# Final-state stores moved to SyncE's queue and sample value products merged by pairs, in a two-layer hybrid decoder step

## The reference, cut to what matters

```python
def block(x, lp, st, ffn_fn, ffn_p):
    mix, new_st = mixer(rmsnorm(x, lp['n1']), lp, st)
    x = x + mix @ lp['w_out']
    x = x + ffn_fn(rmsnorm(x, lp['n2']), *ffn_p)
    return x, new_st
```

```python
    s = jnp.einsum('nthd,ntjhd->nthj', q.astype(F32), kg) * (Dh ** -0.5)
    ...
    o = jnp.einsum('nthj,ntjhd->nthd', p, vg) / den[..., None]
    new_buf = jnp.concatenate([buf, jnp.stack([k, v], axis=2).astype(buf.dtype)], axis=1)[:, T:]
```

## Time and profile before

| what | value |
|---|---|
| median of 3 runs | 1847.91 us |
| the profiled execution | 1849.23 us |
| its span, first to last instruction | 1847.0 us |
| PE busy / DVE / ACT / POOL | 1687.7 / 954.0 / 696.2 / 391.3 us |
| mean granted TensorE clock | 0.936 of full speed |
| mixer's end of layer 0 / layer 1 | about 306 to 352 us / 1088 to 1133 us |

### The profile page before, as it was taken

How to read it: one execution, slowest core, us unless ns; L and a number is a source line. 1 busy time by engine, 2 the same in 40 slices (tenths; PEclk the granted TensorE clock), 3 DMA queues, 4 the chain that set the end, 5 groups by cost and what they waited for, 6 DMA issues and landing times.

```text
span 1847.0 us, 33779 instructions
## 1 busy us (share of the span) xinstructions
PE 1687.7 (91%) x13514; PEld 1625.7 (88%) x13514; DVE 954.0 (52%) x1433; ACT 696.2 (38%) x1050; POOL 391.3 (21%) x236
## 2 busy tenths in 40 slices
PE   6999978799999999998999877859999999999993
PEld 5999857789999999998998567859999999999993
DVE  5577676532210122226776765255746548457474
ACT  4533363342221223235333633443534435335342
POOL 4300250343443344443002503030000000000031
PEclk8999986699999999999999877969999999999997
DMA  4222227422222223222222212368778678677682
GB/s 176 81 70 77 74 72 266 188 80 92 92 87 86 81 92 105 79 81 69 69 77 78 70 50 86 112 211 277 241 246 288 217 255 290 216 266 259 234 313 75
DMA packets 71225, 271.42 MB, mean 147 GB/s; under 512 B 11668, under 2 KB 12404, under 8 KB 70300
## 3 DMA queue, kind: packets, MB, share of 16 engines
q1 hardware_dynamic: 63988, 250.52, 39.7%
q10 hardware_dynamic: 3464, 10.62, 1.8%
q0 software_dynamic: 3648, 8.53, 1.3%
HBM read 253.24 MB, written 36.34 MB: 157 GB/s over the span
## 4 chain that ended last, share of the span: by engine, by line
PE 81%; DVE 7%; POOL 4%; issue 3%; ACT 2%; DMA 1%; ACTq 0%; DVEq 0%; POOLq 0%; SPq 0%
PE psum L1189 39%; PE psum L1709 11%; PE psum L1719 10%; PE psum L1711 9%; PE psum L1236 9%; POOL r_cvt L674 2%; POOL r_w L676 1%; PE psum L1688 1%; PE psum L1241 1%; PE psum L1677 1%; DVE n L1780 1%; POOL r_cvt L675 1%; DVE r_bt L1964 0%; DVE acc L1767 0%; DMA wraw<-in_w_in 0%
## 5 line engine op out<-in xcount | busy, mean ns | idle before, releaser
L1709 PE MATMUL psum<-xg,xhi 128*128 128x320 f32 x1408 | 371.4, 307 | 1.2 <-issue 0.9
L1711 PE MATMUL psum<-xg,xlo 128*128 128x256 f32 x1408 | 369.7, 282 | 0.0
L637 POOL TENSOR_TENSOR wlo<-wraw,whi 128x1024 fp32r<-128x1024 f32 (+1 forms) x90 | 231.3, 2572 | 405.0 <-ACT whi L777 405.0
L1709 PEld LDWEIGHTS psum<-xg,xhi 128*128 128x128 f32 x1408 | 265.2, 188 | 3.5 <-issue 3.1
L1711 PEld LDWEIGHTS psum<-xg,xlo 128*128 128x128 f32 x1408 | 265.3, 188 | 0.0
L1189 PE MATMUL psum<-xnh,whi 128*128 128x260 f32 x1120 | 234.6, 291 | 32.1 <-POOL xnl L694 12.5
L777 ACT CAST whi<-wraw 128x1024 fp32r<-128x1024 f32 (+1 forms) x130 | 140.7, 1085 | 288.4 <-DMA wraw<-in_w_in 161.9
L415 DVE TENSOR_TENSOR xlo<-xraw,xhi 128x1024 fp32r<-128x1024 f32 x176 | 215.2, 1224 | 54.3 <-ACT xhi L1137 54.2
L1137 ACT CAST xhi<-xraw 128x1024 fp32r<-128x1024 f32 x176 | 182.7, 1048 | 142.1 <-PE psum L1711 142.0
L1189 PE MATMUL psum<-xnl,whi 128*128 128x260 f32 x1120 | 228.3, 286 | 0.0
L1189 PE MATMUL psum<-xnh,wlo 128*128 128x260 f32 x1120 | 228.2, 286 | 0.0
(11 more groups left out here) (427 smaller groups left out, 2422.1 us busy)
## 6 DMA issues: line engine op xcount, KB each, us to landing
xraw<-in_moe_gu SPq DMA_DIRECT2D x176, 512.0 KB, 4.2
xraw<-in_moe_dn SPq DMA_DIRECT2D x64, 704.0 KB, 5.8
wraw<-in_w_in SPq DMA_DIRECT2D x54, 512.0 KB, 3.2
wraw<-in_ffn_gu SPq DMA_DIRECT2D x44, 512.0 KB, 3.2
wraw<-in_ffn_dn SPq DMA_DIRECT2D x16, 704.0 KB, 4.1
wraw<-in_w_out SPq DMA_DIRECT2D x16, 512.0 KB, 3.5
out_cache_s<-in_cache SPq DMA_DIRECT2D x4, 2040.0 KB
rows_in<-in_zero SPq DMA_DIRECT2D x8, 640.0 KB, 33.8
```

What stands on the lines that cost most here:

```text
L637: pool.tensor_tensor(wlo[u % RAW][:, 0:cols], wraw[u % RAW][:, 0:cols], whi[u % SPL][:, 0:cols].bitcast(F32), ALU.subtract).then_inc(lo_ma ...
L1709: pe.matmul(epart(n), xhi[n % HIX][:, k * P:(k + 1) * P], xg[:, k, :], start=(k == 0), stop=False, skip_group_check=True)
L1711: ins = pe.matmul(epart(n)[:, 0:256], xlo[n % RWX][:, k * P:(k + 1) * P], xg[:, k, 0:256], start=False, stop=(k == KD - 1), skip_group_che ...
```

## The change

Four edits:

- The six state stores are taken off ACT's list in `sample` and put on SP's, behind a wait for PE's job `mt` 2 and ahead of the cache shifts (layer 0) or the gain tables (layer 1).
- `wv` is moved ahead of the outputs of heads 2 and 3 on PE and in the table of jobs; with that the bank of `wv` and of the next nine jobs changes.
- The 64-row and the 16-row product of each sample become one of 80 rows by 2 x 2 columns: 16 products for 24. For that the probabilities of group 2 go to columns of their own in `spw` (16 columns wider), the rest of these columns is cleared once by POOL, and ACT makes one more small copy per layer.
- DVE adds the result of `wv` (two instructions) before the third `normalise` and not after the last `mean_squares`.

ACT still waits for `state_out` at the end of `sample`, as before.

```diff
@@ mixer_jobs
-    jobs += [..., ("md", 4), ("mqk", 4)]
+    jobs += [..., ("md", 4), ("mqk", 4), ("wv",)]
     jobs += [("mi", 2), ("mi", 3), ("mo", 2), ("mo", 3), ("co", 0), ("co", 1), ("mt", 2), ("mi", 4), ("mo", 4)]
-    jobs += [("wv",), ("mt", 3), ("fx",), ("mt", 4)]
+    jobs += [("mt", 3), ("fx",), ("mt", 4)]
@@ SP
                 sp.dma_start(R["cv"][:], a["cv"][li]).then_inc(state_in, 16)
+                made(sp, li, "mt", 2)
+                for name, src in (("hgrn_p", R["sall"][:, NC - 1, :, :]), ("mlstm_p", R["call"][:, NC, :, :]),
+                                  ("hgrn_s", flat(TQ, 3 * NB * 64)), ("mlstm_s", flat(TSV, 3 * NB * 65)),
+                                  ("m_p", proj[0:5, 5, SEQ - 1:SEQ]), ("m_s", R["sc8"][0:5, 32:40])):
+                    sp.dma_start(a[name][li], src).then_inc(S("state_out"), 16)
                 for n in range(RAW - 1, KD):
@@ POOL
                 bump(pool.memset(R["att"][:], 0.0), S("scratch_clear"), pool)
+                if li == 0:
+                    bump(pool.memset(spw[:, 64:96], 0.0), S("spw_clear"), pool)
@@ ACT
-                    ins = act.copy(spw[0:80, 64:80], bank("wp")[0:80, 64:80])
+                    if li == 0:
+                        act.wait_ge(S("spw_clear"), 1)
+                    step(act.copy(spw[0:64, 64:80], bank("wp")[0:64, 64:80]))
+                    ins = act.copy(spw[64:80, 80:96], bank("wp")[64:80, 64:80])
...
                 taken(act, li, "fx")
-                for name, src in (("hgrn_p", ...), ..., ("m_s", R["sc8"][0:5, 32:40])):
-                    act.dma_start(a[name][li], src).then_inc(S("state_out"), 16)
                 for m in range(KD):
@@ PE
+                def values():
+                    pe.wait_ge(state_in, 64 * (li + 1))
+                    j = Job(li, "wv")
+                    own = spw[0:80, 64:96].rearrange("p (g c) -> p g c", g=2)
+                    for b in range(NB):
+                        c = 2 * b
+                        j.mm(c, 2, R["cv"][:, b, 0, :], spw[:, c:c + 2])
+                        j.last = pe.matmul(j.out(16, 32).rearrange("p (g c) -> p g c", g=2)[:, :, c:c + 2],
+                                           R["cv"][0:80, b, 1, :], own[:, :, c:c + 2], start=True, stop=True,
+                                           skip_group_check=True)
+                    j.end()
...
                 decays((4,))
+                values()
                 outputs((2, 3))
...
                 outputs((4,))
-                pe.wait_ge(state_in, 64 * (li + 1))
-                j = Job(li, "wv")
-                for b in range(NB):
-                    c = 2 * b
-                    j.mm(c, 2, R["cv"][:, b, 0, :], spw[:, c:c + 2])
-                    for g, (r, rows) in ((1, (0, 64)), (2, (64, 16))):
-                        j.mm(16 * g + c, 2, R["cv"][r:r + rows, b, 1, :], spw[r:r + rows, 64 + c:66 + c])
-                j.end()
                 turn_heads(li, 3)
```

More of the change, by code:

```diff
@@ L81, in mixer_jobs @@
     jobs += [("cu", 2), ("cu", 3), ("so", 0), ("so", 1), ("rs",), ("aw",)]
-    jobs += [("md", 2), ("md", 3), ("mqk", 2), ("mqk", 3), ("mi", 0), ("mi", 1), ("mo", 0), ("mo", 1), ("md", 4), ("mqk", 4)]
+    jobs += [("md", 2), ("md", 3), ("mqk", 2), ("mqk", 3), ("mi", 0), ("mi", 1), ("mo", 0), ("mo", 1), ("md", 4), ("mqk", 4), ("wv",)]
     jobs += [("mi", 2), ("mi", 3), ("mo", 2), ("mo", 3), ("co", 0), ("co", 1), ("mt", 2), ("mi", 4), ("mo", 4)]
-    jobs += [("wv",), ("mt", 3), ("fx",), ("mt", 4)]
+    jobs += [("mt", 3), ("fx",), ("mt", 4)]
     return jobs
@@ L153, in program @@
         lbt, _ = at("lbt", [P, 4, 3])
-        spw, _ = at("spw", [P, 80])
+        spw, _ = at("spw", [P, 96])
         st8, _ = at("st8", [P, 3, NB])
@@ L1002, in sample @@
                 taken(act, li, "fx")
-                for name, src in (("hgrn_p", R["sall"][:, NC - 1, :, :]), ("mlstm_p", R["call"][:, NC, :, :]),
-                                  ("hgrn_s", flat(TQ, 3 * NB * 64)), ("mlstm_s", flat(TSV, 3 * NB * 65)),
-                                  ("m_p", proj[0:5, 5, SEQ - 1:SEQ]), ("m_s", R["sc8"][0:5, 32:40])):
-                    act.dma_start(a[name][li], src).then_inc(S("state_out"), 16)
                 for m in range(KD):
@@ L2225, in mlstm @@
                 decayed(4)
-                normalise(li, 3)
-                gate_heads(li, 2)
-                c8_out()
-                finish(4)
-                mean_squares(li, 4)
                 made(v, li, "wv")
@@ L2239, in mlstm @@
                         step(ins)
+                normalise(li, 3)
+                gate_heads(li, 2)
+                c8_out()
+                finish(4)
+                mean_squares(li, 4)
                 gate_heads(li, 3)
```

## The result

The changed kernel takes 1897.07 us (median of 4 runs, 1895.08 to 1898.85) against 1847.98 for the kernel before, measured beside it: a ratio of 1.0264, 95% interval 1.0246 to 1.0281. The profiled execution took 1898.85 us with a span of 1897.0, against 1849.23 and 1847.0.

The account below looks back on a forecast made before the run. PE carried 81% of the chain, so PE's waits were taken to count. 41.1 us in layer 0 plus 0 elsewhere on the profiled 1849.23 gave 1890.3; with the median 1.3 lower, 1889 us, range 1881 to 1898.

Parts of the forecast that it names:

- The products: `wv` on PE: starts about 311.97, 32 instructions instead of 48 take 8.0 us (7.5 to 11.3); `mt` 2 ends at 331.9.
- Six issues: SP's six state stores in layer 0 take 2.6 us to issue, up to 4.4; first cache copy at 334.5.
- 68.0 us to the last landing: Layer 0's 14 cache copies and zero fills need 68.0 us from first issue to last landing, as before: 402.5.
- The 2 us for the stores' bytes: State stores ahead on SP's queue delay layer 0's copies and fills by 2 us (0 to 5.2): 404.5.
- The load behind the last fill: The `w_out` load for unit 3, layer 0's output projection, comes behind the last zero fill and lands at 406.5.
- the load passes the copies: Rival: unit 3's `w_out` load is not held by layer 0's copies; 1849.3 us, no change that can be told; chance 0.06.
- one slow engine is enough: Argument that unit 3's load is held although half the DMA engines are free: a single slow engine can hold it.
- 2.0 us of bytes: Time for all bytes of unit 3's `w_out` load to land once the last zero fill is through.
- Unit 3: Layer 0's output projection: PE starts this unit at 410.1 instead of 370.79, 39.3 us later, plus 1.8 for lower clock.
- Layer 1: Mixer's end there: copies at about 1129.6 against 1130.44, a gain of 0.8, taken as 0 (-2 to +3).
- The rest, put at 0: POOL's one clearing of 32 columns and ACT's extra copy of 16 columns, at most 0.4 per layer, taken as 0.
- The forecast's 41.1: Total loss in layer 0: 39.3 us until PE starts unit 3 of the output projection, plus 1.8 for lower clock.

Follow-up runs that it names:

- other_queue: The changed kernel with layer 0's cache copies and zero fills issued from ACT's queue, wait and state stores staying on SP: 1892.48 us.
- spread: The changed kernel with every cache copy cut so its outermost dimension has 16 pieces instead of 8, plus a small copy for the row between: 1880.82 us.
- fills_first: The changed kernel with layer 0's cache copies and zero fills put ahead of SP's wait for `mt` 2 and the state stores: 1856.64 us.
- old_place: The changed kernel with copies and fills ahead of the wait and stores, and the merged products back behind the outputs of head 4: 1847.77 us.
- the padding: Sixteen idle transposes added per layer to the changed kernel, so that PE's instruction stream has its old length: 1890.75 us.

## Why the prediction was right, and what its sum missed

The sign, the place and the mechanism held, and the time lies in the range, 8 us above the forecast and 1 us below the upper bound. That it lies inside is in part luck: some 12 us came from places for which the sum had a term of 0, and the room for them was that of other terms. Step by step:

- *The products.* They start at 312.57, released by DVE's first read of the scores, as forecast (311.97; this execution was 0.6 us later already). They take 6.9 us, not 8.0, and less than the lower bound of 7.5: at the same lower clock a product of two instructions takes 0.43 us, where an unmerged one took 0.50 (8.00 us for 32 instructions). So the number of products does not decide alone, as the prediction had it. Of the 5.1 us saved at that clock (24 times 0.50 less 16 times 0.43) 4.0 are the number, and 1.1 that each became cheaper. Why it did stays open. `mt` 2 ends at 330.3, not 331.9.
- *Six issues.* 3.9 us from the first to the first copy, not 2.6; within the bound of 4.4. The two errors cancel: copies at 334.21, forecast 334.5.
- *68.0 us to the last landing.* 67.7 (334.2 to 401.9). The 2 us for the stores' bytes did not appear here, and no run shows them apart.
- *The load behind the last fill.* It landed at 403.2, forecast 406.5. The picture was half right: in the records 64 of its 128 packets move at once, at 361 to 363 us, and 64 after 400. So half of the rival "the load passes the copies" came true, and that the other half held it is the answer the prediction gave ("one slow engine is enough"). Its 2.0 us of bytes were too many for half a load. other_queue shows that the queue's order was not needed for it; spread shows that the eight idle engines made up some 15 us of the hold.
- *Unit 3.* 36.1 us late, forecast 39.3. The lower clock behind the stop was forecast at 1.8; the step from 36.1 to 37.7 in the table agrees.
- *Layer 1.* From the first job behind the scores to the output projection 35.04 us, before 34.98: 0, as forecast. So the issues and the third of `wv` were spent as the prediction said; fills_first against old_place, 8.9 us apart with only the values' place changed, shows it from the other side.
- *The rest, put at 0.* This step failed. The forecast's 41.1 were 37.7 up to the feed-forward part; then came 12.3 us more. Of these 5.5 are the 64 bytes by which the wider `spw` moved the tiles behind it, and 3.7 the length of PE's stream; just ahead of that 1.2 were regained, in a stretch that takes 67.7 to 68.1 us in some of the kernels and 69.0 to 69.2 in the others, whatever the stream. "POOL clears 32 columns, ACT copies 16" priced every added instruction and neither the tile's size nor the instructions that were gone. The last 4.3 us, in layer 1, are not settled: part is lower clock there (12.41 us for 34 matmuls that took 10.76), with the padding all of them are gone, but in fills_first, which has no padding, all but 1.0 are gone as well.

## What to carry to other kernels

Before a wait goes into a queue, list everything behind it: 15 MB of copies that nobody needs soon are harmless early and cost 36 us when they are let go just ahead of a weight load, and another queue did not free the load, because the transfers share the DMA engines. An outermost dimension of 8 kept half of those engines idle here (a share of 0.49, against 0.98 with 16). And a kernel that comes out some microseconds off at places the edit doesn't touch may have lost them to its layout: repeat it with the old addresses and the old instruction count before judging the idea; here that turned "no gain" into 1% (0.9904, interval 0.9886 to 0.9922).

## What the runs showed that I had not expected

- 64 bytes in the address of the tiles behind `spw`, the experts' weights among them, make 305 to 307 ns a product into 310, 5 to 6 us over the experts.
- Sixteen matmuls fewer in a layer put a second stop of 2.0 to 2.8 us into a loop far behind them, with lower clock after it that cost 1 to 3 us more.
- A merged product of 80 rows and four columns is no dearer than one of 128 rows and two: 0.43 us each at the lower clock, so 0.86 a batch, where the three unmerged ones took 1.50.
